# Output projections of the first block: two of the three matmuls of each weight tile joined into one of 512 columns, with two additions out of the bank

## The chip, the cores and the metric

The kernel runs on one core of a Trainium2 chip. The metric is device time in microseconds (us) of one execution; the time given for a kernel is the median of several executions. The engines are called PE (TensorE: matmuls), PEld (its weight loads), DVE (VectorE), ACT (ScalarE), POOL (GpSimd) and SP (SyncE, which issues the weight transfers).

## The reference, cut to what matters

Two transformer blocks run one after the other on 256 tokens of width 2048, all in float32. The first block has two layers, and each ends with an output projection, which is what the change touches:

```python
def first_block(x, ...):
    for l in range(DEPTH):                     # DEPTH = 2
        h = rms_norm(x, norm_g[l])
        z = h @ w_in[l]
        ...                                    # 16 heads of attention of three kinds
        y = jnp.concatenate([o_na * jax.nn.silu(na_g), o_dl * jax.nn.silu(dl_g), o_m * jax.nn.silu(m_g)], axis=-1)
        x = x + y @ w_out[l]                   # y: 256 x 2048, w_out[l]: 2048 x 2048
    return rms_norm(x, final_g)
```

The second block (a state-space mixer, an attention, a gated feed-forward part) takes this x.

## The kernel before

**Precision.** Every operand of a float32 matmul is split into a high and a low part, `hi` = the value rounded to the matmul's format and `lo` = the value minus `hi`. A product is w_hi·x_hi + w_hi·x_lo + w_lo·x_hi. Activations lie with the feature on the partitions: tensor `[128, 16, 256]`, 16 feature tiles of 256 tokens.

**Weights.** They come as chunks of 128 x 1024 (eight tiles of 128 x 128, 512 KB) into the ring `w_raw` of four slots. For each chunk ACT rounds to `w_hi` (line 748), then DVE subtracts to `w_lo` (line 1374), then PE uses both; `w_free` gives a slot back to ACT, `w_lo_ready` gives `w_raw`'s slot back to SP. Two chunks make a **job**: one output block of 128 columns, summed over 16 feature tiles `kt`. Four jobs make a period, and job `c` of a period uses the PSUM bank `z_ps[c]`, which holds 2 x 256 float32 per partition.

**Two forms of a job.** `chunk` (lines 2162 to 2164) issues three matmuls of 256 columns for each `kt`: w_hi by hi, w_hi by lo, w_lo by hi, all into one half of the bank. `chunk_joined` (lines 2174 and 2175) needs hi and lo in one tensor (`x_both`, `m_both`: `[P, 2, KT, T]`): one matmul of 512 columns (w_hi by both) into the whole bank, and one of 256 (w_lo by hi) into its first half. The halves of the bank must then be added. The heads of layer 0 and half of the head jobs of layer 1 are joined; the output projections are not.

**Output projection of a layer.** 16 jobs, periods `po` to `po + 3`. The first period is written out by hand around the last head's attention (lines 2344 to 2358): the chunks of jobs 0 and 1 lie between the head's transposes and products, and their last `kt` waits for the last head's y. Jobs 2 and 3 and the periods of `out_rest` follow as plain jobs. In layer 0, `out_rest` is unrolled and PE also builds 8 rows of a bias table between jobs (line 2316); in layer 1 it is a hardware loop.

**The order on ACT and DVE around an output job.** Both engines work through a fixed list: the split of job c+1, then `out_block` of job c-1. On DVE that is `w_lo` twice, then `res += z` (line 1477, waits for the job's matmuls, signals `z_free`), then `x_lo` (line 1479, waits for ACT's `x_hi`). On ACT it is `w_hi` twice (line 748), then `x_hi` from `res` (line 753, waits for `z_free`), in layer 1 a scaled square (line 757), and a square (line 758). POOL adds the squares up (lines 540 and 541). After the last output job of a layer PE sums the squares over the partitions, DVE and ACT make the reciprocal root (`rstd`), and the next stage's results are scaled with it.

Of the kernel before, what the change touches and what calls it, by code (L numbers as in the profile page):

```python
# [9 lines left out]
F32R = mybir.dt.float32r  # L10
# [21 lines left out]
CH = 8  # L32
# [39 lines left out]
def build(nc, ap, out):  # L72
    ctx = ExitStack()
    with ctx:
        def sb(name, shape, dt=F32):
            return ctx.enter_context(nc.sbuf_tensor(name, shape, dt))
# [10 lines left out]
        x_hi, x_lo = x_both[:, 0], x_both[:, 1]  # L87
        m_both = sb("m_both", [P, 2, KT, T], F32R)
        m_hi, m_lo = m_both[:, 0], m_both[:, 1]
        y_hi = sb("y_hi", [P, KT, T], F32R)  # L90
        y_lo = sb("y_lo", [P, KT, T], F32R)
        gains = sb("gains", [P, 4, KT])
        final_g = sb("final_g", [P, KT])
        norm1_w = sb("norm1_w", [P, KT])
# [282 lines left out]
        fa_turned = sem("fa_turned")  # L377
        down_used = sem("down_used")
        down_turned = sem("down_turned")
        turned_added = sem("turned_added")  # L380
        fg_hi = sem("fg_hi")
        fg_lo = sem("fg_lo")
        out_stored = sem("out_stored")
# [880 lines left out]
        def _(dve):  # L1264
# [209 lines left out]

            def out_block(p, c, l, n):
                job_done(p, c)
                dve.tensor_tensor(res[:, n, :], z_ps[c % 4][:, 0, :], res[:, n, :], ALU.add).then_inc(z_free, 1)
                dve.wait_ge(x_hi_ready, (l + 1) * KT + n + 1)
                dve.scalar_tensor_tensor(out=x_lo[:, n, :], in0=res[:, n, :],
                                         scalar=gains_f[:, bass.ds((l + 1) * KT + n, 1)],  # L1480
                                         in1=x_hi[:, n, :].bitcast(F32), op0=ALU.mult,
                                         op1=ALU.subtract).then_inc(x_lo_ready, 1)
# [595 lines left out]
            def add_turned(k):  # L2078

                dve.wait_ge(down_turned, k + 1)  # L2080
                for h in range(2):
                    r = slice(4 * k + 2 * h, 4 * k + 2 * h + 2)
                    e = dve.tensor_tensor(res[:, r, :], z_ps[2 * (k % 2) + h][:], res[:, r, :], ALU.add)
                e.then_inc(turned_added, 1)

            def column_rstd():

# [51 lines left out]
            for k in range(4):  # L2139
                if k < 3:  # L2140
                    ffn_split(N_GROUPS, k + 1)
                if k == 0:
                    ffn_down_rows(ffn_base(N_GROUPS - 1) + 16, N_GROUPS - 2, 3)
                add_turned(k)
                dve.wait_ge(turned_added, k + 1)
                ffn_down(ffn_base(N_GROUPS), N_GROUPS - 1, k)


# [1 line left out]
        def _(pe):  # L2150
# [168 lines left out]
            for l in range(DEPTH):  # L2319
# [22 lines left out]

                attn_scores(po - 1, l, g)
                pe.wait_ge(z_free, 4 * po + 1)
                z, z1 = z_ps[0][:, 0, :], z_ps[1][:, 0, :]
                chunk(z, po, 0, range(CH), y_hi, y_lo, True, False, y_there).then_inc(w_free, 1)
                chunk(z, po, 1, range(CH, HEADS - 1), y_hi, y_lo, False, False, y_there)
                attn_turn(g)
                if l == 1:
                    pe.wait_ge(m_ready, ST)  # L2350
                pe.wait_ge(z_free, 4 * po + 2)
                chunk(z1, po, 2, range(CH), y_hi, y_lo, True, False)
                attn_values(g)
                chunk(z1, po, 3, range(CH, HEADS - 1), y_hi, y_lo, False, False)
                chunk(z, po, 1, [HEADS - 1], y_hi, y_lo, False, True, y_there).then_inc(w_free, 2)
                chunk(z1, po, 3, [HEADS - 1], y_hi, y_lo, False, True).then_inc(w_free, 1)
                for c in range(2, 4):
                    job(po, c, y_hi, y_lo)
                    if l == 0 and c == 2:
                        pe.wait_ge(b_landed, 16)  # L2360
                        turn_b(v_ps)
                def out_rest(i):
                    for c in range(4):
                        job(po + i, c, y_hi, y_lo)
                        if l == 0 and 0 <= 4 * i + c - REL_AT < N_DH:
                            if 4 * i + c == REL_AT + 1:
                                pe.wait_ge(bt_ready, 1)
# [443 lines left out]
```

## Time and profile before

| | |
|---|---|
| time, median of 3 executions | 2445.16 us (2444.61 to 2445.4) |
| span of the profiled execution | 2444.5 us |
| PE busy | 2416.1 us, 99% |
| DVE busy | 1700.9 us, 70% |
| ACT busy | 1219.8 us, 50% |
| POOL busy | 611.5 us, 25% |
| chain of work that ended last: PE / DVE | 83% / 8% |

The profile is of one execution. Busy time of PE is the union of its matmuls' records, and these overlap: a matmul's record is longer than the distance to the start of the next. What a matmul costs in a gapless stretch is read from the distance between starts. In the timeline each row has the start, the duration, the engine, the line and the operation, and in brackets the idle time of the engine before it and who ended it.

### The profile page before, as it was taken

The page shows a single profiled execution, that of the slowest core. Times are in us where ns is not written, and L with a number is a line of the kernel's source. Part 1 is how long each engine was busy: PE and PEld are TensorE (multiplying, and loading weights), DVE is VectorE, ACT ScalarE, POOL GpSimd, SP SyncE. Part 2 cuts the span into 40 slices and gives each one's busy share as a digit, 9 for nine tenths or more (in the row PEclk, how much of TensorE's full clock was granted, in tenths as well). Part 3 has the DMA queues.
Part 4 walks back from the last instruction along what each step waited for, and adds up shares of the span by engine and source line. Part 5 has one row for each costly group of instructions (what it writes and reads, how often), then busy time and mean ns, then how long its engine had stood idle before and what let it go on. Part 6 is the DMA issues. An engine that isn't in the chain of part 4 may idle for free.

```text
span 2444.5 us, 45436 instructions
## 1 busy us (share of the span) xinstructions
PE 2416.1 (99%) x15336; PEld 2179.8 (89%) x15336; DVE 1700.9 (70%) x2649; ACT 1219.8 (50%) x1830; POOL 611.5 (25%) x1003
## 2 busy tenths in 40 slices
PE   8999999999999999999999999999999999999999
PEld 7888888989999999999999999998888888888888
DVE  8977777668877776677878875666555555555555
ACT  5454554456566665566665444344444444444442
POOL 2210031358988884211012221111000000000000
PEclk9999999999999999999999999999999999999999
DMA  7765566656565655556566866665777677777774
GB/s 241 220 204 201 181 225 200 198 178 206 192 201 198 197 194 173 187 168 206 165 196 229 274 221 228 218 196 187 199 192 193 189 190 191 190 190 191 191 190 147
DMA packets 257480, 485.01 MB, mean 198 GB/s; under 512 B 24072, under 2 KB 172244, under 8 KB 257120
## 3 DMA queue, kind: packets, MB, share of 16 engines
q1 hardware_dynamic: 216064, 415.66, 55.2%
q0 software_dynamic: 11296, 32.68, 4.4%
q10 hardware_dynamic: 30016, 35.30, 4.4%
q8 instruction: 63, 1.03, 0.2%
q14 instruction: 41, 0.34, 0.0%
HBM read 455.20 MB, written 31.08 MB: 199 GB/s over the span
## 4 chain that ended last, share of the span: by engine, by line
PE 83%; DVE 8%; issue 3%; ACT 2%; POOL 2%; DMA 1%; ACTq 0%; DVEq 0%; SPq 0%; POOLq 0%
PE z_ps L2174 14%; PE z_ps L2162 9%; PE z_ps L2164 9%; PE z_ps L2163 9%; PE z_ps L2175 7%; PE z_ps L2566 7%; PE z_ps L2567 7%; PE z_ps L2572 7%; DVE w_lo L1374 3%; ACT w_hi L748 1%; PE o_ps L2217 1%; PE s_ps L2199 1%; POOL arena L593 1%; PE p_ps L2601 1%; PE o_ps L2601 1%
## 5 line engine op out<-in xcount | busy, mean ns | idle before, releaser
L1374 DVE TENSOR_TENSOR w_lo<-w_raw,w_hi 128x1024 fp32r<-128x1024 f32 x518 | 633.3, 1249 | 246.8 <-ACT w_hi L748 244.8
L748 ACT ACTIVATE w_hi<-w_raw 128x1024 fp32r<-128x1024 f32 x518 | 531.1, 1051 | 266.2 <-PE z_ps L2175 128.6
L2033 DVE TENSOR_TENSOR w_lo<-w_raw,w_hi 128x1024 fp32r<-128x1024 f32 x262 | 320.8, 1226 | 300.6 <-ACT w_hi L1214 300.5
L2174 PE MATMUL z_ps<-x_both,w_hi 128*128 128x512 f32 x1440 | 517.7, 402 | 7.0 <-DVE w_lo L1374 3.5
L1214 ACT ACTIVATE w_hi<-w_raw 128x1024 fp32r<-128x1024 f32 x262 | 277.7, 1061 | 415.3 <-PE z_ps L2572 267.2
L2162 PE MATMUL z_ps<-x_both,w_hi 128*128 128x256 f32 x1376 | 398.9, 290 | 6.0 <-DVE w_lo L1374 5.4
L2175 PE MATMUL z_ps<-x_both,w_lo 128*128 128x256 f32 x1440 | 403.9, 281 | 0.0
L2164 PE MATMUL z_ps<-x_both,w_lo 128*128 128x256 f32 x1376 | 390.6, 284 | 0.0
L2163 PE MATMUL z_ps<-x_both,w_hi 128*128 128x256 f32 x1376 | 390.5, 284 | 0.0
L2174 PEld LDWEIGHTS z_ps<-x_both,w_hi 128*128 128x128 f32 x1440 | 271.0, 188 | 71.8 <-issue 7.3
L2162 PEld LDWEIGHTS z_ps<-x_both,w_hi 128*128 128x128 f32 x1376 | 265.2, 193 | 11.0 <-issue 8.9
L2566 PE MATMUL z_ps<-w_hi,x_both 128*128 128x512 f32 x704 | 275.0, 391 | 0.0
L2567 PE MATMUL z_ps<-w_hi,x_both 128*128 128x512 f32 x704 | 274.1, 389 | 0.0
L2175 PEld LDWEIGHTS z_ps<-x_both,w_lo 128*128 128x128 f32 x1440 | 272.6, 189 | 0.5
L2163 PEld LDWEIGHTS z_ps<-x_both,w_hi 128*128 128x128 f32 x1376 | 265.2, 193 | 0.5
L2164 PEld LDWEIGHTS z_ps<-x_both,w_lo 128*128 128x128 f32 x1376 | 265.0, 193 | 0.0
L2162 PE MATMUL z_ps<-y_hi,w_hi 128*128 128x256 f32 x736 | 210.4, 286 | 1.8 <-DVE w_lo L1374 1.8
L2163 PE MATMUL z_ps<-y_lo,w_hi 128*128 128x256 f32 x736 | 208.2, 283 | 0.0
L2164 PE MATMUL z_ps<-y_hi,w_lo 128*128 128x256 f32 x736 | 208.2, 283 | 0.0
L2572 PE MATMUL z_ps<-w_lo,x_both 128*128 128x512 f32 x704 | 188.2, 389 | 0.0
L2572 PEld LDWEIGHTS z_ps<-w_lo,x_both 128*128 128x128 f32 x704 | 132.1, 188 | 27.5
L2567 PEld LDWEIGHTS z_ps<-w_hi,x_both 128*128 128x128 f32 x704 | 132.2, 188 | 27.2
(471 smaller groups left out, 4264.2 us busy)
## 6 DMA issues: line engine op xcount, KB each, us to landing
w_raw<-in_w SPq DMA_DIRECT2D x624, 512.0 KB, 4.2
w_raw<-in_w SPq DMA_DIRECT2D x160, 256.0 KB, 3.3
w_raw<-in_w SPq DMA_DIRECT2D x80, 384.0 KB, 4.9
w_raw<-in_w SPq DMA_DIRECT2D x80, 128.0 KB, 3.0
tab_d<-arena ACTq DMA_DIRECT2D x32, 256.0 KB, 2.9
res<-tab_d POOLq DMA_DIRECT2D x16, 384.0 KB, 5.4
arena<-tab_d POOLq DMA_DIRECT2D x16, 384.0 KB, 5.6
tab_d<-arena ACTq DMA_DIRECT2D x32, 128.0 KB, 3.2
```

The costliest lines, as they stand in the source:

```text
L748: act.activation(w_hi[:, n % RING, :], w_raw[:, n % RING, :], ACT.Copy).then_inc(w_hi_ready, 1)
L1214: act.activation(w_hi[:, k % RING, :], w_raw[:, k % RING, :], ACT.Copy).then_inc(w_hi_ready, 1)
L1374: dve.tensor_tensor(w_lo[:, n % RING, :], w_raw[:, n % RING, :], w_hi[:, n % RING, :].bitcast(F32), ALU.subtract).then_inc(w_lo_ready, 1)
L2033: dve.tensor_tensor(w_lo[:, k % RING, :], w_raw[:, k % RING, :], w_hi[:, k % RING, :].bitcast(F32), ALU.subtract).then_inc(w_lo_ready, 1)
L2162: pe.matmul(z, wh, hi[:, kt, :], start=(first and i == 0), stop=False)
L2163: pe.matmul(z, wh, lo[:, kt, :], start=False, stop=False)
L2164: m = pe.matmul(z, wl, hi[:, kt, :], start=False, stop=(last and i == len(kts) - 1))
L2174: pe.matmul(z[:], wh, both[:, :, kt, :], start=(first and kt == kts[0]), stop=False)
L2175: m = pe.matmul(z[:, 0, :], wl, both[:, 0, kt, :], start=False, stop=(last and kt == kts[-1]))
L2566: pe.matmul(z[t], x_hi[:, kt, r], hi_w[:, :, i * P:(i + 1) * P], start=(kt == 0), stop=False)
L2567: pe.matmul(z[t], x_lo[:, kt, r], hi_w[:, :, i * P:(i + 1) * P], start=False, stop=False)
L2572: m = pe.matmul(z[t], x_hi[:, kt, t * P:(t + 1) * P], lo_w[:, :, i * P:(i + 1) * P], start=False, stop=(kt == KT - 1))
```

## The change

`y_hi` and `y_lo` become the two halves of one tensor `y_both`. All 16 output jobs of both layers use `chunk_joined` on it. The bank is emptied by two additions instead of one: the first half into `res`, then, after a wait on the first addition (`res_added`), the second half. Only the second signals `z_free`. The semaphore `turned_added` of the end of the kernel is renamed and its count moved on; nothing else there changes. Uses of `y_hi` and `y_lo` in the second block stay as they are.

```diff
-        y_hi = sb("y_hi", [P, KT, T], F32R)
-        y_lo = sb("y_lo", [P, KT, T], F32R)
+        y_both = sb("y_both", [P, 2, KT, T], F32R)
+        y_hi, y_lo = y_both[:, 0], y_both[:, 1]
...
             def out_block(p, c, l, n):
                 job_done(p, c)
-                dve.tensor_tensor(res[:, n, :], z_ps[c % 4][:, 0, :], res[:, n, :], ALU.add).then_inc(z_free, 1)
+                dve.tensor_tensor(res[:, n, :], z_ps[c % 4][:, 0, :], res[:, n, :], ALU.add).then_inc(res_added, 1)
+                dve.wait_ge(res_added, l * KT + n + 1)
+                dve.tensor_tensor(res[:, n, :], z_ps[c % 4][:, 1, :], res[:, n, :], ALU.add).then_inc(z_free, 1)
                 dve.wait_ge(x_hi_ready, (l + 1) * KT + n + 1)
...
                 attn_scores(po - 1, l, g)
                 pe.wait_ge(z_free, 4 * po + 1)
-                z, z1 = z_ps[0][:, 0, :], z_ps[1][:, 0, :]
-                chunk(z, po, 0, range(CH), y_hi, y_lo, True, False, y_there).then_inc(w_free, 1)
-                chunk(z, po, 1, range(CH, HEADS - 1), y_hi, y_lo, False, False, y_there)
+                chunk_joined(z_ps[0], po, 0, range(CH), y_both, True, False, y_there).then_inc(w_free, 1)
+                chunk_joined(z_ps[0], po, 1, range(CH, HEADS - 1), y_both, False, False, y_there)
                 attn_turn(g)
...
                 pe.wait_ge(z_free, 4 * po + 2)
-                chunk(z1, po, 2, range(CH), y_hi, y_lo, True, False)
+                chunk_joined(z_ps[1], po, 2, range(CH), y_both, True, False)
                 attn_values(g)
-                chunk(z1, po, 3, range(CH, HEADS - 1), y_hi, y_lo, False, False)
-                chunk(z, po, 1, [HEADS - 1], y_hi, y_lo, False, True, y_there).then_inc(w_free, 2)
-                chunk(z1, po, 3, [HEADS - 1], y_hi, y_lo, False, True).then_inc(w_free, 1)
+                chunk_joined(z_ps[1], po, 3, range(CH, HEADS - 1), y_both, False, False)
+                chunk_joined(z_ps[0], po, 1, [HEADS - 1], y_both, False, True, y_there).then_inc(w_free, 2)
+                chunk_joined(z_ps[1], po, 3, [HEADS - 1], y_both, False, True).then_inc(w_free, 1)
                 for c in range(2, 4):
-                    job(po, c, y_hi, y_lo)
+                    pe.wait_ge(z_free, 4 * po + c + 1)
+                    job_joined(z_ps[c], po, c, y_both)
...
                 def out_rest(i):
                     for c in range(4):
-                        job(po + i, c, y_hi, y_lo)
+                        pe.wait_ge(z_free, 4 * (po + i) + c + 1)
+                        job_joined(z_ps[c], po + i, c, y_both)
```

On DVE, one turn of layer 1's loop over the output jobs stands like this before: the split of the next job, the addition (its wait is the ISA row), x_lo.

```order
L1374 TENSOR_TENSOR w_lo<-w_raw,w_hi 128x1024 [waits w_hi_ready]
L1373 REGISTER_ALU
L1374 TENSOR_TENSOR w_lo<-w_raw,w_hi 128x1024 [waits w_hi_ready]
L1477 ISA [waits w_free]
L1477 TENSOR_TENSOR res<-z_ps1,res 128x256
L1478 REGISTER_ALU
L1479 ISA [waits x_hi_ready]
L1479 SCALAR_TENSOR_TENSOR x_both<-res,gains,x_both 128x256
```

And the same turn after the change, where x_lo is line 1481:

```order
L1374 TENSOR_TENSOR w_lo<-w_raw,w_hi 128x1024 [waits w_hi_ready]
L1373 REGISTER_ALU
L1374 TENSOR_TENSOR w_lo<-w_raw,w_hi 128x1024 [waits w_hi_ready]
L1477 ISA [waits w_free]
L1477 TENSOR_TENSOR res<-z_ps1,res 128x256
L1478 REGISTER_ALU
L1479 TENSOR_TENSOR res<-z_ps1,res 128x256 [waits res_added]
L1480 REGISTER_ALU
L1481 ISA [waits x_hi_ready]
L1481 SCALAR_TENSOR_TENSOR x_both<-res,gains,x_both 128x256
```

A second addition stands between the first and x_lo; its wait is part of the instruction, and the register operation for that wait stands ahead of it. Nothing on ACT, POOL or SP has moved.

On PE, the boundary between two output jobs of layer 0 (jobs 4 and 5, with a row of the bias table between) before:

```order
L2162 MATMUL z_ps0<-y_hi,w_hi 128x256
L2163 MATMUL z_ps0<-y_lo,w_hi 128x256
L2164 MATMUL z_ps0<-y_hi,w_lo 128x256
L2316 MATMUL s_ps<-x_both 128x512 [waits rel_split]
L2162 MATMUL z_ps1<-y_hi,w_hi 128x256 [waits w_lo_ready,z_free]
L2163 MATMUL z_ps1<-y_lo,w_hi 128x256
L2164 MATMUL z_ps1<-y_hi,w_lo 128x256
```

And after:

```order
L2176 MATMUL z_ps0<-y_both,w_hi 128x512
L2177 MATMUL z_ps0<-y_both,w_lo 128x256
L2318 MATMUL s_ps<-x_both 128x512 [waits rel_split]
L2176 MATMUL z_ps1<-y_both,w_hi 128x512 [waits w_lo_ready,z_free]
L2177 MATMUL z_ps1<-y_both,w_lo 128x256
```

Three matmuls and three weight loads for each `kt` have become two and two; the waits are the same. There are 2 x 16 x 16 = 512 such groups.

## Rows read from the trace of the kernel before

**Rows 1.** The page, part 1: busy time, share of the span, instructions.
```profile
PE 2416.1 (99%) x15336; PEld 2179.8 (89%) x15336; DVE 1700.9 (70%) x2649; ACT 1219.8 (50%) x1830; POOL 611.5 (25%) x1003
```
**Rows 2.** Two stretches: length, PE, PEld, DVE, ACT, POOL busy, clock, DMA share, GB/s.
```profile
984.00:1056.00 72.00, 72.00 (x602) 72.00 (x601) 47.29 (x52) 39.76 (x65) 18.48 (x26) 1.00 0.57 188
1076.40:1079.70 3.30, 3.30 (x15) 3.30 (x16) 2.92 (x9) 1.46 (x3) 0.00 (x0) 0.50 0.66 207
```
**Rows 3.** Timeline of PE, a split output job of layer 0: first of three.
```profile
459.72 0.28 PE L2162 MATMUL z_ps<-y_hi,w_hi 128*128 128x256 f32 x1
...
462.60 0.28 PE L2162 MATMUL z_ps<-y_hi,w_hi 128*128 128x256 f32 x1
```
**Rows 4.** Timeline of PE, a joined head job of layer 0: first of two.
```profile
299.69 0.39 PE L2174 MATMUL z_ps<-x_both,w_hi 128*128 128x512 f32 x1
...
302.81 0.40 PE L2174 MATMUL z_ps<-x_both,w_hi 128*128 128x512 f32 x1
```
**Rows 5.** Timeline of PE, a joined head job of layer 1: first of two.
```profile
955.18 0.40 PE L2174 MATMUL z_ps<-x_both,w_hi 128*128 128x512 f32 x1
...
958.36 0.40 PE L2174 MATMUL z_ps<-x_both,w_hi 128*128 128x512 f32 x1
```
**Rows 6.** Timeline of DVE, one turn of layer 1's output loop.
```profile
998.33 0.41 DVE L1477 TENSOR_TENSOR res<-z_ps,res 128x256 f32 x1
999.68 0.48 DVE L1479 SCALAR_TENSOR_TENSOR x_both<-res,gains,x_both  x1 [0.95 <-ACT x_both L753]
1001.18 2.84 DVE L1374 TENSOR_TENSOR w_lo<-w_raw,w_hi 128x1024 fp32r<-128x1024 f32 x2 [1.01 <-ACT w_hi L748]
1003.94 0.41 DVE L1477 TENSOR_TENSOR res<-z_ps,res 128x256 f32 x1
```
**Rows 7.** Timeline of ACT, the same turn.
```profile
998.98 0.51 ACT L753 ACTIVATE x_both<-res,gains  x1 [2.50 <-DVE res L1477]
999.39 0.50 ACT L757 ACTIVATE arena<-res,final_g 128x256 f32 x1
999.79 0.40 ACT L758 ACTIVATE arena<-res 128x256 f32 x1
1000.10 1.99 ACT L748 ACTIVATE w_hi<-w_raw 128x1024 fp32r<-128x1024 f32 x2
```
**Rows 8.** Timeline of DVE, start and end of layer 1's output stage.
```profile
979.12 2.85 DVE L1374 TENSOR_TENSOR w_lo<-w_raw,w_hi 128x1024 fp32r<-128x1024 f32 x2 [1.17 <-ACT w_hi L748]
984.53 2.85 DVE L1374 TENSOR_TENSOR w_lo<-w_raw,w_hi 128x1024 fp32r<-128x1024 f32 x2 [1.17 <-ACT w_hi L748]
...
1051.67 2.83 DVE L1374 TENSOR_TENSOR w_lo<-w_raw,w_hi 128x1024 fp32r<-128x1024 f32 x2 [1.03 <-ACT w_hi L748]
...
1059.81 5.01 DVE L1374 TENSOR_TENSOR w_lo<-w_raw,w_hi 128x1024 fp32r<-128x1024 f32 x4 [1.65 <-ACT w_hi L748]
1064.74 0.41 DVE L1393 TENSOR_SCALAR arena<-p_ps 128x256 f32<-128x256 f32 x1
```
**Rows 9.** Timeline of DVE, two operations of which the second waits for the first.
```profile
1067.37 0.43 DVE L1383 TENSOR_TENSOR arena<-arena 128x256 f32<-128x256 f32 x1 [2.21 <-ACT arena L852]
1067.83 0.42 DVE L1385 TENSOR_TENSOR arena<-arena 128x256 f32<-128x256 f32 x1
```
**Rows 10.** Timeline of PE, its two waits around layer 1's output stage.
```profile
980.98 0.36 PE L2162 MATMUL z_ps<-y_hi,w_hi 128*128 128x256 f32 x1 [0.73 <-DVE w_lo L1374]
...
1076.36 0.55 PE L2162 MATMUL z_ps<-x_both,w_hi 128*128 128x256 f32 x1 [2.16 <-DVE w_lo L1374]
```
**Rows 11.** Timeline of DVE, layer 0's output stage: splits for jobs 4 and 5.
```profile
443.05 2.36 DVE L1374 TENSOR_TENSOR w_lo<-w_raw,w_hi 128x1024 fp32r<-128x1024 f32 x2 [2.33 <-ACT w_hi L748]
...
448.61 2.36 DVE L1374 TENSOR_TENSOR w_lo<-w_raw,w_hi 128x1024 fp32r<-128x1024 f32 x2
```
**Rows 12.** Timeline of PE, first matmuls of jobs 4 and 5 of layer 0.
```profile
444.44 0.33 PE L2162 MATMUL z_ps<-y_hi,w_hi 128*128 128x256 f32 x1
...
450.75 0.39 PE L2162 MATMUL z_ps<-y_hi,w_hi 128*128 128x256 f32 x1
```

More of the change, by code:

```diff
@@ L379, in build @@
         down_turned = sem("down_turned")
-        turned_added = sem("turned_added")
+        res_added = sem("res_added")
         fg_hi = sem("fg_hi")
@@ L2083, in add_turned @@
                     e = dve.tensor_tensor(res[:, r, :], z_ps[2 * (k % 2) + h][:], res[:, r, :], ALU.add)
-                e.then_inc(turned_added, 1)
+                e.then_inc(res_added, 1)
             def column_rstd():
@@ L2144, in _ @@
                 add_turned(k)
-                dve.wait_ge(turned_added, k + 1)
+                dve.wait_ge(res_added, DEPTH * KT + k + 1)
                 ffn_down(ffn_base(N_GROUPS), N_GROUPS - 1, k)
```

## The prediction

> **What bounds the kernel now.** I read the page first: PE is busy 99% of the span [rows 1], so by the shares alone anything that relieves PE should pay. In layer 1's output stage PE is busy all of the 72 us from 984 to 1056, at a granted clock of 1.00 (2.4 GHz) [rows 2]. But a full PE does not say how far away the next bound is, so I read the timeline twice more: for what the two forms of a job cost PE, and for the pace of the engines that feed it.
>
> **The pace of PE.** The records overlap (0.28 us long, but 0.12 us apart), so I use distances between starts. Split: eight groups of three matmuls from 459.72 to 462.60, 2.88 / 8 = 0.360 us for each kt [rows 3]. Joined: nine groups of two from 299.69 to 302.81, 3.12 / 9 = 0.347 us [rows 4]; in another stretch nine groups in 3.18 us, 0.353 us [rows 5]. Both paces occur, each for whole jobs, and I can't tell from the trace which the output jobs would get. So joining saves PE 0.007 to 0.013 us for each kt; I take the middle, 0.010. A job of 16 kt falls from 5.76 to between 5.55 and 5.65 us, and all 512 groups together could give 3.4 to 6.8 us, no more: the columns stay 768, and only the cost of starting a third matmul goes.
>
> First the row: a split matmul of 256 columns costs 0.120 us [rows 3]. The Trainium skill, "TensorE: Matmul & The Clock Gate", section "Back-to-back issue gap", has columns divided by 2.4 GHz plus 2.5 ns, by which it would be 109 ns, and joining would save only 2.5 ns for each kt, an estimate by that page; the rows disagree, and they decide. By the page the gain counted below for layer 0 would be 0.4 us in place of 1.8, and the sum 2452.0 us.
>
> **The pace of the feeders.** This is the step on which I rest the forecast. In layer 1's output loop, follow one turn [rows 6, 7]: DVE adds the bank into res (998.33); ACT waits for just that and makes x_hi (998.98), two squares (999.39, 999.79), then w_hi of the next-but-one job (1000.10); DVE waits for w_hi and makes w_lo twice (1001.18), and only then comes to the next addition (1003.94). Each step waits for the one before it, and the turn closes on itself: 1003.94 - 998.33 = 5.61 us. PE is not in it. PE needs 5.76 us a job, so the turn is hidden with 0.15 us to spare, and its DVE and ACT look idle (47.3 and 39.8 of 72 us [rows 2]) only because they wait for each other. In the three jobs ahead of the loop the turn is 984.53 - 979.12 = 5.41 us [rows 8].
>
> **The change, part by part.** *Second addition.* It stands between the first and z_free, and z_free is what ACT waits for, so all of it lies on the turn. Price: two DVE operations of this size, the second waiting for the first, start 1067.83 - 1067.37 = 0.46 us apart with a first one of 0.43; with 0.41 for the addition that is 0.45 us. Bounds: below, 0.41, its bare duration; above, 0.65, if register work for its loop-dependent addresses falls behind the wait, as at x_hi, which starts 998.98 - 998.74 = 0.24 us after the addition ends [rows 6, 7] where a hand-over without register work costs 0.03 [rows 9]. I take 0.45, because here the wait is part of the instruction and the register operation stands ahead of it. *Wait on res_added.* Queued behind it on DVE are x_lo and the splits; for whom they matter is counted in the turn. *y_both, the renamed semaphore.* Nothing: same bytes, same operations. *Transfers.* No transfer moves; a slot of raw weights is filled again after its w_lo, two jobs ahead of use, and the stage draws 188 GB/s [rows 2].
>
> *Layer 1.* The turn becomes 5.61 + 0.45 = 6.06 us (5.86 in the first jobs), more than PE's 5.55 to 5.65 and also more than the 5.76 of before. PE now waits some 0.4 us in every job, and how fast it is no longer counts. w_lo of job 16 (the first of the next stage) is behind additions 0 to 13, so its start moves from 1051.67 [rows 8] by 14 x 0.45 = 6.3 us. What ends the stage is the chain to rstd: after w_lo of job 16 comes addition 14, then 15, the squares, w_hi and four w_lo (1059.81), and the first step of rstd behind them in DVE's queue (1064.74) [rows 8]. Addition 14 delays the square and the w_hi once more; addition 15's own 0.45 falls on x_hi, and ACT's next square waits for POOL anyway. So this chain moves by 15 x 0.45 = 6.8 us. PE waits for its end already (2.16 us at 1076.36 [rows 10]), so the whole shift reaches PE and the end. From it goes 0.15 us: the chain starts when PE gives back the ring slots of jobs 0 and 1, and 16 groups, joined now, lie between PE's last wait for DVE and that point (16 x 0.010). Sum of layer 1: +6.6 us.
>
> *Layer 0.* No scaled square and no loop, so the turn there is shorter, and from job 5 PE sets the pace. The start is tight, though. The split for job 4 starts at 443.05; one w_lo takes 1.2 us and PE could start some 0.2 later; it did start at 444.44 [rows 11, 12]. Additions 0 and 1 move that by 0.9 less 0.15. The split for job 5 starts at 448.61, behind three additions: 448.61 + 1.2 + 0.2 + 1.35 - 0.15 = 451.2; PE coming from job 4 needs 444.44 + 0.75 + 6.31 (the distance in rows 12) less 0.16 (16 kt by 0.010) = 451.35, the later of the two. So job 5 starts 0.6 us later than its 450.75 [rows 12]. Then 11 jobs by 16 kt by 0.010 give back 1.8 us (1.2 to 2.3). Sum of layer 0: -1.2 us (-0.6 to -1.7). The first 15 kt of each stage I count at nothing: behind them PE waits for the last head's probabilities, whose chain over DVE and ACT starts at that head's scores.
>
> *Total.* 6.6 - 1.2 = +5.4 us on the profiled execution's span of 2444.5, that is 2449.9; the median of the runs is 0.7 us above the span, and I carry the difference over: 2445.2 + 5.4 = 2450.6 us.
>
> **The rivals.** *(A) The forecast: the turn of ACT and DVE takes over in layer 1.* 2450.6. For it: the turn can be followed in rows, and its margin is 0.15 us against 0.45 added.
> *(B) PE stays the bound throughout.* If the turn had slack that I don't see (ACT running ahead of the addition, say), both layers gain: 3.4 to 6.8 us less some 1 us at the starts, 2441. It decides at an added time of 0.04 us or less. Against it: ACT's wait of 2.50 us before x_hi ends with the addition in every turn [rows 7].
> *(C) Slower still.* The second addition costs 0.65 us in the loop's 12 turns: 12 x 0.2 = 2.4 us more, 2453.0. Against it is only the place of the register operation.
> *(D) The loss is masked.* The joined jobs of layer 1's heads run at 0.353 [rows 5]; if moved waits put them on the 0.347 pace, 32 jobs by 16 kt by 0.0065 us give 3.3 us: 2447.3, no measurable change. Nothing in the trace says that they would; in the other direction there is nothing to lose, since those jobs are at the slow pace already.
> *(E) The records mean what they say.* 0.28 + 0.28 us become 0.40, 512 times: 80 us faster. The overlap in rows 3 and 4 excludes it almost wholly.
> A smaller unknown: after the wait at 1076.36 PE works 3.3 us at a granted clock of 0.50, that is 1.2 GHz [rows 2], 15 matmuls where some 27 would fit, a loss of 1.4 us. The wait there grows from 2.2 to about 3.5 us, and such a stretch may come twice or not at all: 1.4 us either way, which both ends of the range hold.
>
> **How the numbers follow.** Chances: A 0.62, B 0.09, C 0.13, D 0.15, E 0.01. From 0.41 for an addition (15 x 0.04 = 0.6 less) to 0.65, and layer 0 between its bounds, A and C span 2449.5 to 2453.6. With D and 0.7 us of scatter for the clock the range is 2447.0 to 2454.3; outside are B, E and the tails, some 2 in 10. A measurement of this kernel can tell about 0.2%, 4.9 us, from no change, and that line, 2450.1, runs close under the forecast: of A I give 0.68 to slower and the rest to no change; C is slower; D is no change; of B one third passes 0.2%. Slower 0.42 + 0.13 + 0.01 = 0.56, faster 0.03 + 0.01 = 0.04, same 0.40.
>
> **What the profile after would show.** Right: in layer 1 additions 6.0 to 6.1 us apart, the second 0.45 behind the first; PE with a wait for w_lo ahead of each output job from job 3 to job 16, about 0.4 us each; in layer 0 gapless jobs from job 5 on at 0.347 to 0.353 for each kt. Wrong: no PE waits in layer 1 (B); additions more than 0.55 apart (C); layer 1's heads at 0.347 (D). The forecast falls as a whole if ACT makes w_hi without having waited for the second addition.

## The result, and the profile after

The changed kernel takes 2453.27 us (median of 6, 2451.75 to 2454.53) where the kernel before, measured beside it, takes 2445.39 us (6, 2444.61 to 2448.23). The ratio is 1.0031, 95% interval 1.0021 to 1.0042. It is slower, by 5 to 10 us, and 2.7 us above the predicted 2450.6. The span of the profiled execution went from 2444.5 to 2451.4 us.

Busy time answers [rows 1]: PE has 512 matmuls fewer, and is not less busy for it.

```profile
PE 2418.1 (99%) x14824; PEld 2154.0 (88%) x14824; DVE 1712.9 (70%) x2681; ACT 1218.9 (50%) x1830; POOL 612.7 (25%) x1003
```

By windows, the stretch of layer 1's output stage that [rows 2] shows of before (columns as there). PE was busy all 72 us; now 1.9 us are missing, with 384 matmuls where 602 stood. The second line is the stretch at half clock behind the stage, 6.8 us long instead of 3.4.

```profile
984.00:1056.00 72.00, 70.11 (x384) 58.25 (x383) 48.85 (x60) 36.77 (x60) 16.99 (x24) 1.00 0.53 174
1081.20:1088.00 6.80, 5.77 (x27) 5.80 (x28) 6.42 (x14) 2.82 (x5) 0.71 (x2) 0.50 0.45 154
```

Timeline of DVE, one turn of layer 1's output loop, which answers [rows 6]. Line 1477 is the first addition, line 1479 the second.

```profile
999.21 0.41 DVE L1477 TENSOR_TENSOR res<-z_ps,res 128x256 f32 x1
999.66 0.42 DVE L1479 TENSOR_TENSOR res<-z_ps,res 128x256 f32 x1
...
1002.53 2.83 DVE L1374 TENSOR_TENSOR w_lo<-w_raw,w_hi 128x1024 fp32r<-128x1024 f32 x2 [1.02 <-ACT w_hi L748]
1005.28 0.41 DVE L1477 TENSOR_TENSOR res<-z_ps,res 128x256 f32 x1
```

And ACT in the same turn, which answers [rows 7]:

```profile
1000.33 0.51 ACT L753 ACTIVATE x_both<-res,gains  x1 [2.96 <-DVE res L1479]
...
1001.45 1.99 ACT L748 ACTIVATE w_hi<-w_raw 128x1024 fp32r<-128x1024 f32 x2
```

Read it as a ring. The second addition starts 0.45 us behind the first. ACT now waits 2.96 us for line 1479, where it waited 2.50 for line 1477. From first addition to first addition it is 1005.28 - 999.21 = 6.07 us instead of 5.61. The order of the steps is the same, and each still waits for the one ahead of it.

DVE at the start and the end of the stage, which answers [rows 8]:

```profile
978.62 1.70 DVE L1374 TENSOR_TENSOR w_lo<-w_raw,w_hi 128x1024 fp32r<-128x1024 f32 x1 [1.17 <-ACT w_hi L748]
...
1057.10 2.84 DVE L1374 TENSOR_TENSOR w_lo<-w_raw,w_hi 128x1024 fp32r<-128x1024 f32 x2 [1.02 <-ACT w_hi L748]
...
1070.61 0.41 DVE L1393 TENSOR_SCALAR arena<-p_ps 128x256 f32<-128x256 f32 x1
```

From the first split to the first step of rstd it is 91.99 us; before it was 1064.74 - 979.12 = 85.62.

What PE does about it: the first matmul of an output job (timeline), and one row of its waits (waits of PE over the whole kernel: us in total, times, longest).

```profile
1022.48 0.50 PE L2176 MATMUL z_ps<-y_both,w_hi 128*128 128x512 f32 x1 [0.26 <-DVE w_lo L1374]
```

```profile
PE z_ps L2176 <- DVE w_lo L1374: 6.4, 11, 2.3
```

Line 2176 serves the head jobs too, and most of the sum lies at the start of the kernel; in layer 1's output stage (window 975 to 1062) it is 2.6 us in 7 waits, the longest of 1.28 us at 980.47, where before it was 0.7 us in one. The brackets show only the longer of these waits and less than all of each, since the record of the matmul before runs on. By starts, 1022.48 - 1021.94 = 0.54 us lie between this matmul and the one before it, where 0.12 is the pace: 0.42 us lost. Such a distance, of 0.41 to 0.55 us, stands ahead of each job from job 6 (998.21) to job 16 (1058.90), eleven in a row; before there is none of over 0.31 in these jobs.

Layer 0: DVE's splits for jobs 4 and 5 and PE's starts of them, which answer [rows 11, 12], and PE's pace in the place of [rows 3] (first of two matmuls, eight groups apart).

```profile
443.84 2.36 DVE L1374 TENSOR_TENSOR w_lo<-w_raw,w_hi 128x1024 fp32r<-128x1024 f32 x2 [2.33 <-ACT w_hi L748]
...
449.85 2.36 DVE L1374 TENSOR_TENSOR w_lo<-w_raw,w_hi 128x1024 fp32r<-128x1024 f32 x2
```

```profile
445.21 0.47 PE L2176 MATMUL z_ps<-y_both,w_hi 128*128 128x512 f32 x1 [0.76 <-DVE w_lo L1374]
...
451.36 0.50 PE L2176 MATMUL z_ps<-y_both,w_hi 128*128 128x512 f32 x1
...
459.81 0.39 PE L2176 MATMUL z_ps<-y_both,w_hi 128*128 128x512 f32 x1
...
462.58 0.39 PE L2176 MATMUL z_ps<-y_both,w_hi 128*128 128x512 f32 x1
```

Here 2.77 / 8 = 0.346 us for each kt. Other output jobs go at 0.353.

**Where the time went.** I cut both traces at the same events of PE and took the differences of the stretches between them: the first and the last matmul on y of each layer (419.49 and 518.70, 961.18 and 1055.80 before), and the restart behind the wait that rstd ends (547.29, 1076.36).

| stretch | after less before, us | predicted |
|---|---|---|
| start of the kernel to layer 0's output jobs | 0.0 | 0 |
| layer 0's output jobs (to its last matmul) | -0.85 | -1.2 |
| from there to PE's restart after rstd (547) | +0.71 | 0 |
| heads of layer 1, to its output jobs | -0.68 | 0 |
| layer 1's output jobs and the chain to rstd, to PE's restart | +6.68 | +6.6 |
| from there on (the half-clock stretch) | +1.04 | 0 (1.4 either way) |
| sum | +6.9 | +5.4 |

### The profile page after: what moved, and what is told of

Same layout as the page of the kernel before. It is cut to its first block, busy times and chain, and to the rows that moved or that the text cites. A ratio compares the mean times of both kernels' runs of the same rounds, so it can differ in the third digit from the quotient of the medians.

```text
span 2451.4 us, 44484 instructions
## 1 busy us (share of the span) xinstructions
PE 2418.1 (99%) x14824; PEld 2154.0 (88%) x14824; DVE 1712.9 (70%) x2681; ACT 1218.9 (50%) x1830; POOL 612.7 (25%) x1003
## 4 chain that ended last, share of the span: by engine, by line
PE 85%; DVE 9%; ACT 3%; issue 3%; DMA 0%; ACTq 0%; DVEq 0%; SPq 0%; POOL 0%; POOLq 0%
PE z_ps L2176 18%; PE z_ps L2177 9%; PE z_ps L2164 8%; PE z_ps L2166 7%; PE z_ps L2165 7%; PE z_ps L2569 7%; PE z_ps L2570 7%; PE z_ps L2575 7%; DVE w_lo L1374 4%; ACT w_hi L748 1%; PE o_ps L2219 1%; PE s_ps L2201 1%; PE p_ps L2604 1%; PE o_ps L2606 1%; PE o_ps L2604 1%
## 5 line engine op out<-in xcount | busy, mean ns | idle before, releaser
L2176 PE MATMUL z_ps<-y_both,w_hi 128*128 128x512 f32 x512 | 184.2, 403 | 4.2 <-DVE w_lo L1374 3.6
L2570 PEld LDWEIGHTS z_ps<-w_hi,x_both 128*128 128x128 f32 x704 | 132.2, 188 | 27.2
L2569 PEld LDWEIGHTS z_ps<-w_hi,x_both 128*128 128x128 f32 x704 | 132.2, 188 | 27.1
L2177 PE MATMUL z_ps<-y_both,w_lo 128*128 128x256 f32 x512 | 143.2, 280 | 0.0
```

The source lines that it names most:

```text
L2176: pe.matmul(z[:], wh, both[:, :, kt, :], start=(first and kt == kts[0]), stop=False)
L2177: m = pe.matmul(z[:, 0, :], wl, both[:, 0, kt, :], start=False, stop=(last and kt == kts[-1]))
L2569: pe.matmul(z[t], x_hi[:, kt, r], hi_w[:, :, i * P:(i + 1) * P], start=(kt == 0), stop=False)
L2570: pe.matmul(z[t], x_lo[:, kt, r], hi_w[:, :, i * P:(i + 1) * P], start=False, stop=False)
```

## The experiments

Eleven runs of ten kernels. Times stand beside the kernel before on the same chip: 2445.83 us for the step alone, the joined matmuls alone, the first addition off the turn and both moves; 2446.25 for the third step, the two runs with the squares late and the first run of layer 0 alone; 2445.73 for layer 1 alone, layer 0 once more and the copy moved. "Stage" is layer 1's output stage with the chain to rstd, as in the table above, against before. "..." in an edit stands for lines left out, among them the matching counts of the semaphore at the end of the kernel.

**A second step alone, no joined matmul.** The kernel before, with one dependent operation more on DVE:

```diff
-                dve.tensor_tensor(res[:, n, :], z_ps[c % 4][:, 0, :], res[:, n, :], ALU.add).then_inc(z_free, 1)
+                dve.tensor_tensor(res[:, n, :], z_ps[c % 4][:, 0, :], res[:, n, :], ALU.add).then_inc(turned_added, 1)
+                dve.wait_ge(turned_added, l * KT + n + 1)
+                dve.tensor_tensor(res[:, n, :], res[:, n, :], res[:, n, :], ALU.max).then_inc(z_free, 1)
...
```

> The kernel before with its split matmuls, and one more dependent DVE operation of the size of the second addition (res = max(res, res)) between the addition and z_free, in both layers. Theory (the turn of ACT and DVE): turns of layer 1 6.06 us apart in place of 5.61, PE waits for w_lo in every job from 3 to 16 of layer 1, 15 x 0.455 = 6.8 us more there and 0.9 us more at the start of layer 0: 7.7 us slower, 2453.1. Rival (the 512-column matmuls or their traffic cause the loss): no change, 2445.4.

Measured: 2453.99 us (5 runs, 2451.8 to 2455.04), ratio 1.0035 [1.0021, 1.0049]. Timeline of DVE:

```profile
1014.51 0.41 DVE L1477 TENSOR_TENSOR res<-z_ps,res 128x256 f32 x1
...
1020.58 0.41 DVE L1477 TENSOR_TENSOR res<-z_ps,res 128x256 f32 x1
```

The turn is 6.07 us, the stage +7.06. The step by itself, with PE's work as it was, costs what the whole change costs. In this profile no half-clock stretch follows the stage (1.3 us less from there on than before), and layer 0, from its first output job to layer 1's, takes 2.1 us more, where in the changed kernel it takes 0.8 less.

**The joined matmuls alone.** The changed kernel without the second addition, so w_hi·y_lo is missing from its result:

```diff
-                dve.tensor_tensor(res[:, n, :], z_ps[c % 4][:, 0, :], res[:, n, :], ALU.add).then_inc(res_added, 1)
-                dve.wait_ge(res_added, l * KT + n + 1)
-                dve.tensor_tensor(res[:, n, :], z_ps[c % 4][:, 1, :], res[:, n, :], ALU.add).then_inc(z_free, 1)
+                dve.tensor_tensor(res[:, n, :], z_ps[c % 4][:, 0, :], res[:, n, :], ALU.add).then_inc(z_free, 1)
...
```

> The changed kernel with the second addition left out, so w_hi by y_lo is missing from the output projections. Theory: the turn is 5.61 us again; PE's 5.55 to 5.65 no longer bounds layer 1 clearly, and the chain to rstd behind layer 1 hangs on the turn, not on PE, so layer 1 gains only the 0.15 us of its start; layer 0 gains some 240 kt by 0.009 = 2.2 us: 2.3 us faster, 2443.1. Rival (the matmuls bound both layers once the addition is gone): 512 x 0.009 = 4.7 us faster, 2440.7. Rival (joined matmuls cause the loss): slower than 2450.

Measured: 2446.39 us (11 runs, 2442.8 to 2451.16), ratio 1.0005 [0.9996, 1.0014]. Timeline of DVE:

```profile
1012.00 0.41 DVE L1477 TENSOR_TENSOR res<-z_ps,res 128x256 f32 x1
...
1017.62 0.41 DVE L1477 TENSOR_TENSOR res<-z_ps,res 128x256 f32 x1
```

The turn is back at 5.62 us, and the loss is gone. In layer 1 there is no gain either, as expected: the stage is 0.23 us shorter, no more. PE does its jobs faster (-1.52 us to its last output matmul) and then waits longer for rstd (+1.29), because the turn of 5.6 us sets when rstd comes. So in layer 1 joining was worth almost nothing from the start. The 2.2 us expected of layer 0 are not in the median, whose interval reaches from 1.0 us faster to 3.4 slower; in the profile layer 0 is 1.27 us shorter, from its first output job to layer 1's.

**One step more.** The changed kernel with a third dependent operation in the turn (it changes no value):

```diff
-                dve.wait_ge(res_added, l * KT + n + 1)
-                dve.tensor_tensor(res[:, n, :], z_ps[c % 4][:, 1, :], res[:, n, :], ALU.add).then_inc(z_free, 1)
+                dve.wait_ge(res_added, 2 * (l * KT + n) + 1)
+                dve.tensor_tensor(res[:, n, :], z_ps[c % 4][:, 1, :], res[:, n, :], ALU.add).then_inc(res_added, 1)
+                dve.wait_ge(res_added, 2 * (l * KT + n) + 2)
+                dve.tensor_tensor(res[:, n, :], res[:, n, :], res[:, n, :], ALU.max).then_inc(z_free, 1)
...
```

> The changed kernel with one more dependent DVE operation of the same size (res = max(res, res)) between the second addition and z_free. Theory: the cost is linear in what stands on the turn: layer 1 turns of 6.52 us, 15 x 0.455 = 6.8 us more there and 0.5 to 1.4 us more at the start of layer 0, where the turn still stays under PE's job: 7.3 to 8.2 us over the changed kernel, 2461.5. Rival (half of the changed kernel's loss is something else, paid once): 2457 to 2458.

Measured: 2464.28 us (5 runs, 2463.3 to 2467.38), ratio 1.0076 [1.0062, 1.009], span 2461.5. Timeline of DVE:

```profile
1011.88 0.41 DVE L1477 TENSOR_TENSOR res<-z_ps,res 128x256 f32 x1
1012.33 0.42 DVE L1479 TENSOR_TENSOR res<-z_ps,res 128x256 f32 x1
1012.78 0.42 DVE L1481 TENSOR_TENSOR res<-res  x1
...
1018.41 0.41 DVE L1477 TENSOR_TENSOR res<-z_ps,res 128x256 f32 x1
```

The turn is 6.53 us and the stage +13.76, so the third step added 13.76 - 6.68 = 7.1 us: 15.7 times 0.45. Every turn passes its whole step on to the end. The time is 2.8 us above the 2461.5 expected. That lies in layer 0, which takes 4.3 us more than in the changed kernel, where 0.5 to 1.4 were expected: 1.3 in its jobs, and 2.8 between its last output matmul and the restart behind rstd, where PE now waits 2.71 us for w_lo at 528.73. From that restart on this profile is 1.3 us shorter than the changed kernel's.

**The first addition taken off the turn.** In the changed kernel it moves on DVE ahead of the w_lo splits of the next job, where DVE used to wait for w_hi; only the second addition stays behind them. `out_first` holds the wait for the job and the first addition, `out_block` the second addition and x_lo; the hand-written period is changed alike:

```diff
...
+                        out_first(po + i, c - 1, l, 4 * i + c - 1)
                         split_lo(po + i, c + 1)
                         out_block(po + i, c - 1, l, 4 * i + c - 1)
...
```

> The changed kernel complete, with the first addition moved ahead of the split of w_lo in DVE's list, where DVE waits for ACT anyway; the second stays. Theory: the first addition leaves the turn, which is 5.61 us again: as with the second addition left out, about 2443. Rival (the loss is the added DVE time or the matmuls, wherever they stand): stays at 2453.

Measured: 2444.51 us (11 runs, 2442.2 to 2447.7), ratio 0.9998 [0.9989, 1.0007]. Timeline of DVE (line 1481 is the second addition here, line 1477 the first one of the next block):

```profile
1010.32 0.41 DVE L1481 TENSOR_TENSOR res<-z_ps,res 128x256 f32 x1
...
1012.20 0.42 DVE L1477 TENSOR_TENSOR res<-z_ps,res 128x256 f32 x1
1013.17 2.83 DVE L1374 TENSOR_TENSOR w_lo<-w_raw,w_hi 128x1024 fp32r<-128x1024 f32 x2 [0.55 <-ACT w_hi L748]
1015.92 0.41 DVE L1481 TENSOR_TENSOR res<-z_ps,res 128x256 f32 x1
```

Both additions are done, as in the changed kernel, and the turn is 5.60 us. All that differs is where one of them stands. This excludes the work of the addition (DVE's load, its traffic to the bank) as the cause: it was its place on the ring. At 5.60 the turn again sets layer 1's stage (-0.22), and there joining gains nothing; layer 0 is 1.6 us shorter in this profile.

**The squares taken off the turn.** In the changed kernel ACT's two squares of a block move behind the next w_hi splits. `squares` holds them, `out_block` keeps x_hi alone:

```diff
...
                         split_hi(po + i, c + 1)
+                        squares(l, 4 * i + c - 2)
                         out_block(po + i, c - 1, l, 4 * i + c - 1)
...
```

> The changed kernel complete, both additions together as in the change, but in ACT's list the squares stand behind the next split of w_hi. Theory: the squares' 0.7 us leave the turn, 6.06 becomes 5.35, under PE's 5.55 to 5.65: PE bounds layer 1 again, and nearly all of what the two moves together gave is kept, 0.45 less: 2441.3. Rival (only the addition's own place matters): 2444.5, as with the first addition moved, or slower.

Measured: 2441.04 us (11 runs, 2439.48 to 2443.91), ratio 0.9979 [0.997, 0.9988]. Timeline of ACT:

```profile
1009.97 0.51 ACT L753 ACTIVATE x_both<-res,gains  x1 [1.58 <-DVE res L1487]
...
1012.28 1.06 ACT L748 ACTIVATE w_hi<-w_raw 128x1024 fp32r<-128x1024 f32 x1 [0.85 <-PE z_ps L2185]
```

ACT's w_hi now waits for PE to give a slot back. Additions stand 5.65 us apart, which is 16 kt at the pace of 0.353: PE bounds the loop. The stage is 2.73 us shorter than before. Of the gain in time some 1.2 us may be the clock: no half-clock stretch follows the stage in this profile, nor in the next two, and PE's wait there is 1.6 to 1.7 us, where before it was 2.16. But two other runs show none behind waits of 2.16 and 3.07 us, so the shorter wait is not shown to be the reason.

**Both moves,** first addition early and squares late. On DVE and on ACT:

```diff
...
+                        out_first(po + i, c - 1, l, 4 * i + c - 1)
                         split_lo(po + i, c + 1)
...
                         split_hi(po + i, c + 1)
+                        squares(l, 4 * i + c - 2)
...
```

> As the one before, and in ACT's list the squares of an output block stand behind the next split of w_hi. Theory: the turn loses the first addition (0.45) and the squares (0.7): about 4.9 us, well under PE's 5.6, so PE bounds both layers and the joined matmuls pay: layer 1 13 x 0.16 + 1 us of the wait at its start, about 3 us, layer 0 2 us: 2440.4. Rival (some other bound near 5.6 to 5.7 in layer 1, such as the weights' transfers): no better than about 2443.

Measured: 2440.75 us (11 runs, 2437.8 to 2445.65), ratio 0.9983 [0.9974, 0.9992]. Timeline of DVE:

```profile
1012.46 0.42 DVE L1485 TENSOR_TENSOR res<-z_ps,res 128x256 f32 x1 [1.02 <-PE z_ps L2190]
...
1018.02 0.42 DVE L1485 TENSOR_TENSOR res<-z_ps,res 128x256 f32 x1 [1.13 <-PE z_ps L2190]
```

The first addition now waits for PE itself, 5.56 us apart (the pace of 0.347), and the stage is 4.56 us shorter. Against the run with the squares alone the time is no different that I can tell.

**The squares late in the kernel before.** The same `squares` on ACT, in the kernel before, with its three matmuls and one addition:

```diff
...
                         split_hi(po + i, c + 1)
+                        squares(l, 4 * i + c - 2)
                         out_block(po + i, c - 1, l, 4 * i + c - 1)
...
```

> The kernel before (three matmuls of 256 columns, one addition) with the squares behind the next split of w_hi. Theory: the turn is about 4.9 us, but PE needs 5.76 us a job, so only the wait of 1.0 us at the start of layer 1's stage goes: 1.0 us faster, 2444.8; the other 4 us of the kernel with both moves come from the joined matmuls, which pay only once the turn is out of the way. Rival (the moves alone give the gain): 2441.

Measured: 2443.03 us (11 runs, 2441.06 to 2445.94), ratio 0.9987 [0.9978, 0.9996]. Timeline of DVE:

```profile
1010.89 0.42 DVE L1485 TENSOR_TENSOR res<-z_ps,res 128x256 f32 x1
...
1016.65 0.42 DVE L1485 TENSOR_TENSOR res<-z_ps,res 128x256 f32 x1
```

5.76 us apart: the split jobs' 16 x 0.360. The time is 3.2 us under the kernel before, where 1.0 was expected. The stage is 1.50 us shorter: 0.95 to its last output matmul, where the wait at its start (0.73 us before) is gone, and 0.55 in the chain to rstd, which I had not counted; another 1.2 us is the missing half-clock stretch. Beside the kernel with the same move and joined matmuls (2441.04, same chip) it is 2.0 us slower. The scatter of eleven runs of each leaves that open between about 0 and 3 us, but the two profiles agree with it: joining shortens layer 0 by 0.85 us and layer 1's stage by 1.23. That is what it is worth here once the turn is out of the way.

**Layer 1 alone.** The changed kernel with layer 0's output stage as before; on DVE:

```diff
-                dve.tensor_tensor(res[:, n, :], z_ps[c % 4][:, 0, :], res[:, n, :], ALU.add).then_inc(res_added, 1)
-                dve.wait_ge(res_added, l * KT + n + 1)
-                dve.tensor_tensor(res[:, n, :], z_ps[c % 4][:, 1, :], res[:, n, :], ALU.add).then_inc(z_free, 1)
+                dve.tensor_tensor(res[:, n, :], z_ps[c % 4][:, 0, :], res[:, n, :], ALU.add).then_inc(res_added if l == 1 else z_free, 1)
+                if l == 1:
+                    dve.wait_ge(res_added, n + 1)
+                    dve.tensor_tensor(res[:, n, :], z_ps[c % 4][:, 1, :], res[:, n, :], ALU.add).then_inc(z_free, 1)
...
```

> The changed kernel with layer 0's output stage as it was before (three matmuls, one addition); only layer 1 is changed. Turn theory: layer 1's stage alone carries the loss, +6.7 us as in the changed kernel's stages (adds 6.06 apart), and layer 0 gives nothing back, so 2446.0 + 6.7 = 2452.7, not less than the changed kernel by more than its scatter. Rival (the two layers help or hurt each other across the boundary): a sum of the two halves that differs from the whole by over 2 us.

Measured: 2453.23 us (5 runs, 2452.96 to 2455.72), ratio 1.0035 [1.0022, 1.0049]; turns of 6.06 us, stage +6.67. The whole loss is in layer 1, and leaving layer 0 as it was costs nothing that shows. Its 7.5 us and the 0.6 or 0.7 of layer 0 alone, below, add up to the 7.9 of the whole within the scatter.

**Layer 0 alone.** The reverse: one form and one addition in layer 1, the change in layer 0:

```diff
...
+                def y_job(p, c):
+                    if l == 0:
+                        pe.wait_ge(z_free, 4 * p + c + 1)
+                        job_joined(z_ps[c], p, c, y_both)
+                    else:
+                        job(p, c, y_hi, y_lo)
...
```

> The change in layer 0 alone: layer 1's output projection is that of the kernel before (three matmuls, one addition). Theory: layer 0 reaches layer 1's output stage 0.8 us earlier, as in the trace of the changed kernel, and layer 1 costs what it did: 0.8 us faster, 2445.0, no measurable change; turns of 5.61 us in layer 1. Rival (layer 0's half of the change costs as well): at or above 2447.

Measured: 2446.82 us (11 runs, 2444.88 to 2448.76), ratio 1.0003 [0.9993, 1.0012]. No gain, where I had expected 0.8 us. Its output jobs did get shorter, by 0.75 us. The trace shows what followed, on DVE and then PE:

```profile
517.56 0.42 DVE L1477 TENSOR_TENSOR res<-z_ps,res 128x256 f32<-128x256 f32 x1 [1.41 <-PE z_ps L2178]
...
523.79 0.20 DVE L1607 COPY ssm_em<-arena 128x32 f32<-128x32 f32 x1 [4.28 <-DMA arena<-in_cols]
...
524.28 2.50 DVE L1374 TENSOR_TENSOR w_lo<-w_raw,w_hi 128x1024 fp32r<-128x1024 f32 x2
```

```profile
525.78 0.47 PE L2177 MATMUL z_ps<-x_both,w_hi 128*128 128x512 f32 x1 [1.70 <-DVE w_lo L1374]
```

Between layer 0's last block and the first split of layer 1, DVE copies a small table, and this copy waits for a transfer that ACT issues only behind the last block's x_hi (before, x_hi starts at 519.48 and the first of the table's four issues at 519.88). Here is the same place before the change, and after it:

```profile
519.02 0.42 DVE L1477 TENSOR_TENSOR res<-z_ps,res 128x256 f32<-128x256 f32 x1 [1.98 <-PE z_ps L2164]
...
523.06 0.20 DVE L1604 COPY ssm_em<-arena 128x32 f32<-128x32 f32 x1 [2.55 <-DMA arena<-in_cols]
...
523.55 2.36 DVE L1374 TENSOR_TENSOR w_lo<-w_raw,w_hi 128x1024 fp32r<-128x1024 f32 x2
```

```profile
518.18 0.42 DVE L1477 TENSOR_TENSOR res<-z_ps,res 128x256 f32<-128x256 f32 x1 [1.42 <-PE z_ps L2177]
518.64 0.42 DVE L1479 TENSOR_TENSOR res<-z_ps,res 128x256 f32<-128x256 f32 x1
...
522.71 0.20 DVE L1606 COPY ssm_em<-arena 128x32 f32<-128x32 f32 x1 [2.58 <-DMA arena<-in_cols]
...
523.19 2.36 DVE L1374 TENSOR_TENSOR w_lo<-w_raw,w_hi 128x1024 fp32r<-128x1024 f32 x2
```

From the last block's first addition to the first split it was 4.53 us, and is 5.01. PE comes to the boundary 0.84 us earlier, the split only 0.36. The second addition stands ahead of x_hi, of the transfer and of everything behind it.

**Layer 0 alone, once more,** the same kernel without any edit, for the late landing:

> Layer 0 alone once more, the same kernel as e3_layer0_only, for one thing: in the profile of e3 the copy of the ssm columns on DVE waited 4.28 us for its transfer (2.5 to 2.9 in all the others), and PE then stood 1.70 us behind it at the start of layer 1. If that late landing was chance, the wait here is 2.5 to 2.9 us, PE has no stall near 524, and the span of the layer 0 part is 0.8 us shorter than before: 2445.4. If the earlier end of layer 0 makes it late, it recurs: 2446.8.

Measured: 2446.42 us (11 runs, 2444.3 to 2448.82), ratio 1.0005 [0.9996, 1.0014]. The copy waited 2.90 us this time, so the 4.28 was one execution's. PE still stood 0.28 us in front of the split:

```profile
525.31 0.47 PE L2177 MATMUL z_ps<-x_both,w_hi 128*128 128x512 f32 x1 [0.28 <-DVE w_lo L1374]
```

By stretches: output jobs -0.84 us, then +0.77 to the restart at 547. The gain is made and given back at the boundary. The time agrees with the first run of it, against the 2445.4 that I had expected of an ordinary landing.

**Layer 0 alone, the copy moved behind the first split of layer 1:**

```diff
                 if not (norm and l == 0):
                     split_lo(p, 1)
+                if norm and l == 1:
+                    dve.wait_ge(consts_landed, (7 + STEP) * 16)
+                    chain(dve.tensor_copy(d_col.rearrange("p (c s) -> p s c", s=SPC), d_in))
+                    chain(dve.memset(tab_out[:, 2 * P:3 * P], 0.0))
...
-                if l == 1:
-                    dve.wait_ge(consts_landed, (7 + STEP) * 16)
-                    chain(dve.tensor_copy(d_col.rearrange("p (c s) -> p s c", s=SPC), d_in))
-                    chain(dve.memset(tab_out[:, 2 * P:3 * P], 0.0))
```

> Layer 0 alone, with the copy that waits for the transfer (and the memset after it) moved on DVE behind the first split of layer 1. If this copy is what eats layer 0's gain at the boundary, w_lo starts 0.6 us earlier, PE never waits near 524 whatever the landing, and the time is 0.5 to 1.5 us under that of e3: 2445. If the gain is eaten ahead of it (the last block's second addition stands before x_hi, the transfers' issue and w_hi on ACT), the restart near 547 stays within 0.3 us of before: 2445.6 to 2446.

Measured: 2445.39 us (11 runs, 2443.28 to 2448.71), ratio 0.9998 [0.9989, 1.0007]. Timeline of DVE:

```profile
517.39 0.42 DVE L1477 TENSOR_TENSOR res<-z_ps,res 128x256 f32<-128x256 f32 x1 [1.41 <-PE z_ps L2178]
...
521.80 2.36 DVE L1374 TENSOR_TENSOR w_lo<-w_raw,w_hi 128x1024 fp32r<-128x1024 f32 x2 [2.46 <-ACT w_hi L748]
524.08 0.29 DVE L1525 COPY ssm_em<-arena 128x32 f32<-128x32 f32 x1
```

The split follows the addition by 4.41 us, PE has no wait there, and from the last output matmul to the restart only 0.34 us of the 0.84 are given back, against 0.77. That speaks for both parts that I had named: the copy about 0.4 us, the second addition ahead of ACT's issue the rest. The joined matmuls alone, which have the copy there but no second addition, also give back only 0.28 us there. But each is one profile, and in the two kernels that leave layer 0 as it was (the squares late in the kernel before, layer 1 alone) the same stretch moved by -0.03 and +0.28 by itself, so the split into these parts is a reading, not shown. In time the three layer 0 runs can't be told apart with certainty.

## Why the prediction was right in kind and 2.7 us short

**What bounds.** Right: a PE busy for the whole stage did not mean that PE decided. The turn of ACT and DVE did; with the step alone the loss was whole, and with one addition moved out of the turn it was gone. Rival B falls with that, and with the run of the joined matmuls alone. Rival E falls too: PE's busy time did not shrink by 80 us, it went from 2416.1 to 2418.1.

**The price of the step.** Forecast 0.45 us, measured 0.44 to 0.46; the turn 6.06, measured 6.07. Rival C (0.65) did not occur: the register operation ahead of the second addition costs nothing in the loop.

**Layer 1.** Forecast +6.6 us, measured +6.68, +6.67 with layer 1 alone. Within it, w_lo of job 16 is 1057.10 - 960.38 = 96.72 us behind the start of the output jobs, against 1051.67 - 961.18 = 90.49 before: +6.2, where 6.3 was forecast. The waits of PE are near the forecast size (0.29 to 0.43 us lost where 0.4 was forecast), but not ahead of each job from 3 on: job 3's, which was there before with 0.73 us, is 1.28; jobs 4 and 5, which PE reached late, have none that the brackets show; then each has one from job 6. That changes nothing in the sum, which the chain sets.

**Layer 0.** Its jobs started as worked out: job 4 0.77 us later, job 5 at 451.36 (forecast 451.35). Here two terms were off. *The gain of a kt.* From job 5 to the next stage's first matmul, 176 kt gave back 68.07 - 66.62 = 1.45 us, 0.008 us each instead of 0.010, since a part of the jobs ran at 0.353. *The boundary.* I had let the stage's end carry straight into layer 1, and never followed the last block's additions there. They stand ahead of ACT's x_hi, its issue of the transfers and its w_hi, so the 0.84 us arrived as 0.36 at the split and as 0.12 at the restart. This is the step that failed: "sum of layer 0: -1.2 us" measured +0.6 and +0.7 in the two runs of layer 0 alone, each with an interval of about 2.3 us to either side, so the times by themselves hardly exclude it; the traces show the gain going at the boundary. In the profiled execution a part came back among layer 1's heads (-0.68), where PE before stood idle for 0.35 us at 569; in the runs of layer 0 alone that stretch gave 0.14 and 0.55. With layer 0 left as it was, in the run of layer 1 alone, the heads took 0.30 more. I can't say what sets it. That the changed kernel's layer 0 comes to -0.8 in the table, not far from -1.2, is in part luck.

The Trainium skill, "TensorE: Matmul & The Clock Gate", section "Back-to-back issue gap", would by its rule of columns over 2.4 GHz plus 2.5 ns give layer 0's 176 kt 0.4 us, an estimate by that page. The same section says what the prediction left out: that this rule is for an isolated matmul, and that it counts too little at few columns where each matmul has its weight load. The trace agrees with that: 256 columns go at 0.120 us [rows 3], not at 0.109. It gave 1.45 us for the 176 kt, so the rows were the better source, though still an optimistic one.

**Rival D.** Layer 1's heads stayed at 0.353; nothing was masked.

**The clock.** The half-clock stretch behind layer 1's stage was 6.8 us long instead of 3.4 in this execution, and cost 1.04 us; in the prediction it was an unknown of 1.4 either way. With layer 1 alone it was 3.4, and with the step alone there was none, behind a wait as long, so the longer stretch does not come with the longer stage each time.

**The offset.** I added the 0.7 us by which the median stood above the profiled span. In every execution after, time less span is 1.6 to 1.8 us (2453.11 and 2451.4 for the profiled one). The 0.7 had mixed two executions. With 1.5 us in the span (0.4 from layer 0, 1.0 from the clock, 0.1 from layer 1), 1.0 here and 0.2 between profiled run and median the 2.7 are accounted for.

## What to carry to other kernels

In a loop where two in-order engines wait for each other, add up one whole turn from start to start, and compare it with the bound engine's time for a job: a margin of 0.15 us was hidden under a PE that looked 100% busy, and a step of 0.45 us put on the turn cost 15 times itself. Before adding an operation, look for the wait in which it could stand: the same addition ahead of the splits cost nothing, and taking other work off the turn (the squares, which nobody waits for soon) turned a loss of 0.3% into a gain of 0.2% over the kernel before, of which 0.1% came with the squares alone, without the joined matmuls. A gain at the end of a stage must be followed through the next boundary: what stands in the last block's queue goes on to the next stage, and here it ate most of the gain in the runs of layer 0 alone.

## What the runs showed of the hardware that I had not expected

- A pair of matmuls (512 and 256 columns, each with its weight load) goes at 0.346 us or at 0.353 us, mostly whole jobs at one or the other, at a granted clock of 1.00; in one loop it was 5.65 us a job, with one more move on DVE 5.56. What selects the pace stays open.
- The stretches at a granted clock of 0.50 (1.2 GHz) near waits of PE are 3.4 or 6.8 us long or missing at one and the same place, from profile to profile: behind layer 1's output stage 3.4 us long before, 6.8 in the changed kernel, and none in five of the eleven profiles of the experiments. Where it was missing PE took 1.3 to 1.5 us less for the 40 matmuls from its restart on. In the run with the third step it was there (1078.85 to 1082.26), but fell into PE's waiting ahead of the restart at 1093.64, and cost nothing behind it.
- A small transfer whose copy waits 2.5 to 2.9 us in eleven profiles took at least 1.4 us longer in one (4.28), and PE stood for 1.70 us. Single executions of one kernel lie up to 8 us apart (2442.8 to 2451.16 for the joined matmuls alone), so effects near 1 us were read from stretches of the traces, not from times. Part of the scatter arises ahead of all that was changed: layer 0's output jobs begin at 417.79 to 422.07 us in the thirteen profiles.
